# A hybrid attention, convolution and expert layer: one in-projection pass for blocks 4 to 7, and a last pass of only attention, output and peers

## The reference

```
h  = rmsnorm(x)
q, k, v, xc, B, C = split(h @ W_in)          # six parts of 512 columns
sb = stick_breaking(norm(q), norm(k), v)     # 8 heads x 64, causal, query blocks of 128
cv = B * causal_conv3(C * xc)                # 512 channels, 3 taps
x  = x + concat(rmsnorm(sb), rmsnorm(cv)) @ W_out
x  = x + peer(rmsnorm(x))
```

## Time and profile before

| | |
|---|---|
| median of 3 runs | 2881.12 us (2879.61 to 2883.12) |
| profiled execution | 2882.13 us, span 2880.3 us |
| busy: PE, DVE, ACT, POOL | 77%, 69%, 38%, 38% of the span |
| DMA | 1183.9 MB, mean 411 GB/s |
| mean granted TensorE clock | 0.894 |

### The profile page before, as it was taken

The page is one execution under the profiler, slowest core; times in us unless marked ns, Lnnn a source line. Parts: engine busy times, 40 slices in busy tenths (PEclk is TensorE's granted clock), DMA queues, the critical chain, the costliest instruction groups (busy, mean ns, idle before and its releaser), DMA issues. The chain is left out here.

```text
span 2880.3 us, 29917 instructions
## 1 busy us (share of the span) xinstructions
PE 2223.3 (77%) x9210; PEld 1010.4 (35%) x9210; DVE 1984.2 (69%) x4782; ACT 1094.2 (38%) x3164; POOL 1099.2 (38%) x1037
## 2 busy tenths in 40 slices
PE   9888989778986987778886888777898555555555
PEld 6535625333542343333542244333354111111111
DVE  3757766787667678787767666888676666666654
ACT  2333423552333335562333334666233322222222
POOL 0233433343333334443344333554334444434442
PEclk9999999989999998999998799999999787777787
DMA  9899999999999999999999999999999999999998
GB/s 389 333 418 412 398 419 419 417 403 416 387 422 420 419 419 414 414 419 412 407 421 421 420 411 419 406 421 414 419 408 421 419 421 417 420 418 415 418 421 353
DMA packets 178866, 1183.89 MB, mean 411 GB/s; under 512 B 19857, under 2 KB 21521, under 8 KB 47633
## 3 DMA queue, kind: packets, MB, share of 16 engines
q0 software_dynamic: 147456, 1073.81, 90.4%
q1 hardware_dynamic: 31248, 108.17, 9.5%
HBM read 1177.70 MB, written 4.19 MB: 410 GB/s over the span
## 5 line engine op out<-in xcount | busy, mean ns | idle before, releaser
L1471 DVE CUSTOM_DVE_ANT_0 ring<-ring,h2r 128x1024 f32<-128x1024 f32 x1024 | 1248.4, 1223 | 784.9 <-DMA ring<-table_uv,idx_t 778.9
L642 POOL DMA_INDIRECT ring<-table_uv,idx_t x1024 | 1097.3, 1072 | 1761.9 <-DVE dots L1471 1105.4
L910 PE MATMUL acc<-ring,wmask 128*64 128x512 f32 x4096 | 1199.0, 714 | 586.9 <-ACT wmask L1068 584.7
L910 PEld LDWEIGHTS acc<-ring,wmask 128*64 128x64 f32 x4096 | 282.2, 153 | 1299.9 <-ACT wmask L1068 859.9
L1063 ACT ACTIVATE dots<-dots 128x2 f32<-128x2 f32 x512 | 104.0, 203 | 1514.9 <-DVE dots L1471 1508.4
L1068 ACT ACTIVATE wmask<-gmask,dots 128x64 f32<-128x64 f32 x1024 | 300.3, 340 | 48.6 <-ACT dots L1063 1.5
L1056 ACT ACTIVATE gmask<-stack,gate_t 128x64 f32<-128x64 f32 x1024 | 293.1, 334 | 0.1
L665 PE MATMUL pt<-hT,w_held 128*128 128x256 f32 (+1 forms) x560 | 110.3, 347 | 0.0
L665 PEld LDWEIGHTS pt<-hT,w_held 128*128 128x128 f32 x560 | 89.0, 195 | 27.5 <-issue 20.2
L1063 ACT ACT_TABLE_LOAD x73 | 93.7, 1283 | 1.3
L656 PE MATMUL pz<-w_ring,hT 128*128 128x512 f32 x192 | 90.8, 615 | 0.0
(11 more groups left out here) (274 smaller groups left out, 2167.8 us busy)
## 6 DMA issues: line engine op xcount, KB each, us to landing
w_ring<-wstream SPq DMA_DIRECT2D x121, 512.0 KB
ring<-wstream SPq DMA_DIRECT2D x32, 512.0 KB, 12.2
ring<-table_uv,idx_t POOLq DMA_INDIRECT x1024
w_held<-wstream SPq DMA_DIRECT2D x11, 512.0 KB, 13.7
xs<-x_in_dram SPq DMA_DIRECT2D x8, 512.0 KB
h2r<-wstream SPq DMA_DIRECT2D x8, 512.0 KB
scores<-wstream SPq DMA_DIRECT2D x8, 512.0 KB
xs<-wstream SPq DMA_DIRECT2D x4, 512.0 KB
```

What stands on the lines that cost most here:

```text
L642: nc.gpsimd.indirect_dma_start(out=ring[:, cell(t):cell(t) + 2, :].rearrange("p c d -> p (c d)"), out_offset=None, in_=table, in_offset=ba ...
L910: mm = nc.tensor.matmul(acc[HALF * i:HALF * i + HALF, half * 512:(half + 1) * 512], wmask[:, slot, :], ring[:, cell(2 * p + i) + 1, half * ...
L1471: V.tensor_tensor_reduce(u, u, h2r[:, b % H_SLOTS, i, :], 1.0, 0.0, ALU.mult, ALU.add, dots[:, t % SLOTS:t % SLOTS + 1]).then_inc(dots_don ...
```

## The change

Pass 3 (`WIDE`) makes the in-projection of blocks 4 to 7. Each of its pieces 0 to 23 is done in four parts: the first two for blocks 4 and 5, the last two for blocks 6 and 7 (`AHEAD`). The order of its pieces is q, k, the convolution's, then v. Pass 4 (`LAST`) has only pieces 24 to 47.

The x of blocks 6 and 7 is loaded a second time, ahead, into room that two pieces of `w_held` had (`lent`: a second half of `cvT` and of `qT`); in passes 3 and 4 these two pieces, 37 and 38, are streamed, and in pass 3 so are 33 and 36. The transposed h of blocks 6 and 7 lies in the parts of `kT` and `vals_sb` that their own k and v will fill. The convolution works on 512 tokens at a time in pass 3, and one slot of the scores holds its input. Slots of the scores are numbered anew. Streamed pieces come to 103: 39 in pass 3, 15 in pass 4. The table puts the in-projection of pass 3 at ticks 286 to 366, its 16 attention passes at 369 to 442, its output pieces at 445 to 457 and its peer pieces from 465; pass 4 has its 16 attention passes at 524 to 670, output pieces at 676 to 699, and peer pieces from 715.

```diff
-WHEN = [(-1, -1, 10), (8, 66, 84), (72, 224, 262), (262, 470, 514), (521, 732, 775)]
+WIDE, LAST = 3, 4
+AHEAD = range(FIRST[LAST], BLOCKS)
+WHEN = [(-1, -1, 10), (8, 66, 84), (72, 224, 262), (262, 474, 514), (524, 732, 775)]
...
+ORDER = [list(range(PIECES)) for _ in SUPER]
+ORDER[WIDE] = [*range(PIECE_V), *range(PIECE_CONV, PIECE_OUT), *range(PIECE_V, PIECE_CONV), *range(PIECE_OUT, PIECES)]
+ORDER[LAST] = list(range(PIECE_OUT, PIECES))
...
+def parts_of(f, j):
+    return 4 if f == WIDE and j < PIECE_OUT else SUPER[f]
...
-    if j >= FIRST_HELD:
+    if j >= FIRST_HELD + LENT or j >= FIRST_HELD and f < WIDE:
         return "held", j - FIRST_HELD
...
+    if f == WIDE:
+        main += [(1.0, ("norm", b)) for b in AHEAD]
+        main += [pause(1), (6.0, ("root1", blocks[0])), pause(4)]
+        for pair in (blocks, AHEAD):
+            main += [(2.0, ("h_scale", b)) for b in pair]
+        for pair in (blocks, AHEAD):
+            main += [pause(1)] + [(3.0, ("h", b)) for b in pair] + [(3.0, ("hT", b)) for b in pair]
+        main += [pause(1)] + w(*range(PIECE_K)) + [pause(1)] + w(*range(PIECE_K, PIECE_V)) + [pause(1)]
+        main += [(1.0, ("qk_square", b)) for b in blocks] + w(12) + [(6.0, ("qk_root", blocks[0]))] + w(13)
+        main += [(3.0, ("qk_scale", b)) for b in blocks] + [pause(1)] + [(3.0, ("qk_turn", b)) for b in blocks]
+        main += [(1.0, ("qk_square", b)) for b in AHEAD] + w(14)
+        main += [(6.0, ("qk_root", AHEAD[0]))] + [(3.0, ("qk_scale", b)) for b in AHEAD] + [(8.0, ("conv", 0))]
+        for c in range(1, CH):
+            j = PIECE_CONV + 3 * c
+            main += w(j, j + 1, j + 2) + [(8.0, ("conv", c))]
+        main += w(*range(PIECE_V, PIECE_CONV)) + [pause(1)] + [(3.0, ("qk_turn", b)) for b in AHEAD]
+    elif f == LAST:
+        pass
...
             def front(f, name, *args):
+                if name == "ahead":
+                    sp.wait_ge(piece_done, done(f - 1, FIRST_HELD + LENT - 1))
+                    for i, b in enumerate(AHEAD):
+                        sp.dma_start(lent[i], x[b * P:(b + 1) * P, :]).then_inc(ahead_in, 16)
...
-                blocks = range(0 if begins else 1, n if ends else 1)
-                ks = range(0 if begins else KD // 2, KD if ends else KD // 2)
+                blocks = range(part, part + 1)
+                ks = range(part % n * KD // n, (part % n + 1) * KD // n)
...
+            def product_waits_ahead(f, j):
+                if j == PIECE_K:
+                    pe.wait_ge(q_kept, f + 2)
+                if j == PIECE_V:
+                    pe.wait_ge(cv_ready, 4 * f + 4)
...
                     act.wait_ge(piece_done, done(f, args[0]))
-                    wait(act, u_ready, 4 * f + c)
+                    wait(act, cv_ready if f == WIDE else u_ready, 4 * f + c)
```

More of the change, by code:

```diff
@@ L42 @@
 HELD = 11
+LENT = 2
 EARLY = 32
@@ L94, in cell, with done, made_by, made @@
     return -t * pow(U_HOLD, -1, TURN) % TURN
+ORDER = [list(range(PIECES)) for _ in SUPER]
+ORDER[WIDE] = [*range(PIECE_V), *range(PIECE_CONV, PIECE_OUT), *range(PIECE_V, PIECE_CONV), *range(PIECE_OUT, PIECES)]
+ORDER[LAST] = list(range(PIECE_OUT, PIECES))
+def done(f, j):
+    return sum(len(ORDER[g]) for g in range(f)) + ORDER[f].index(j) + 1
+def made_by(f):
+    return min(f, WIDE)
+def made(f):
+    return 4 if f == WIDE else SUPER[f]
+def made_to(f):
+    return min(BLOCKS, FIRST[made_by(f)] + made(made_by(f)))
+def parts_of(f, j):
+    return 4 if f == WIDE and j < PIECE_OUT else SUPER[f]
 def home(f, j):
-    if j >= FIRST_HELD:
+    if j >= FIRST_HELD + LENT or j >= FIRST_HELD and f < WIDE:
         return "held", j - FIRST_HELD
@@ L106, in home @@
         kind, room = divmod(j - FIRST_ROOM, 3)
-        if f <= room + 1:
+        if f <= min(room + 1, WIDE - 1):
             return ("vals", "keys")[kind], room + 1
     return "stream", 0
-STREAM = [(f, j) for f in range(len(SUPER)) for j in range(PIECES) if home(f, j)[0] == "stream"]
+STREAM = [(f, j) for f in range(len(SUPER)) for j in ORDER[f] if home(f, j)[0] == "stream"]
 PLACED = ([(0, j) for j in range(FIRST_HELD, PIECES)] + [(1, j) for j in range(SPARE)]
@@ L121, in piece_at, with front_head @@
     return j
+def front_head(n, blocks, pause, w):
+    main = [pause(1), (6.0, ("root1", blocks[0])), pause(6)]
+    main += [(2.0, ("h_scale", b)) for b in blocks] + [pause(2)]
+    main += [(3.0, ("h", b)) for b in blocks] + [(3.0, ("hT", b)) for b in blocks] + [pause(4)]
+    main += w(*range(PIECE_V)) + [(1.0, ("qk_square", b)) for b in blocks] + w(8)
+    main += [(6.0, ("qk_root", blocks[0]))] + w(9, 10) + [(3.0, ("qk_scale", b)) for b in blocks] + w(11)
+    return main
 def front_steps(f):
@@ L130, in w @@
     def w(*pieces):
-        if n == 1:
-            return [(piece, ("w", j)) for j in pieces]
-        return [(piece / 2, (half, j)) for j in pieces for half in ("v", "w")]
+        return [(piece / n, ("w", j) if part == parts_of(f, j) - 1 else ("v", j, part))
+                for j in pieces for part in range(parts_of(f, j))]
     def pause(ticks):
         return 0.0, ("pause", ticks)
-    main = [(1.0, ("norm", blocks[0]))]
-    for b in blocks[1:]:
+    main = [(0.0, ("ahead",))] if f == WIDE else []
@@ L140, in front_steps @@
+    main += [(1.0, ("norm", blocks[0]))] if f != LAST else []
+    for b in blocks[1:] if f != LAST else ():
         main += [pause(X_LATE if b >= X_SLOTS + 2 else 0), (1.0, ("norm", b))]
[L141 to L145, removed]
+    if f == WIDE:
[16 more added lines that the diff above has]
+        pass
+    else:
+        main += front_head(n, blocks, pause, w)
@@ L146, in front_steps @@
     conv = []
-    for c in range(CH):
+    for c in range(CH) if f < WIDE else ():
         j = PIECE_CONV + 3 * c
@@ L185, in front_steps @@
                 main += [(6.0, ("stick", *turns[s - 1]))]
-            if s == 1:
+            if s == 1 and f != LAST:
                 main += [(2.0, ("conv_sum",))]
@@ L791, in front @@
                     small_bank("sums")
-                    for t in range(n):
-                        for c in range(CH):
+                    rows, step = (CH, 256) if f < WIDE else (2, 512)
+                    for t in range(made(f)):
+                        for c in range(rows):
                             mm = nc.tensor.matmul(sum_cols[:, t:t + 1],
-                                                  squares[:, c * 256 + t * P:c * 256 + (t + 1) * P], ones[:],
-                                                  start=(c == 0), stop=(c == CH - 1))
+                                                  squares[:, c * step + t * P:c * step + (t + 1) * P], ones[:],
+                                                  start=(c == 0), stop=(c == rows - 1))
                     mm.then_inc(cv_ss, 1)
@@ L941, in front @@
                 i = b - b0
-                if name == "norm":
+                if name == "norm" and i > 1:
+                    act.wait_ge(ahead_in, 32)
+                    act.wait_ge(piece_done, done(f - 1, PIECES - 1))
+                    nc.scalar.activation(spare[i - 2], lent[i - 2], ACT.Square, accum_out=ss1[:, i:i + 1]).then_inc(x_squared, 1)
+                elif name == "norm":
                     act.wait_ge(x_in[b % 2], 16 * (b // 2 + 1))
@@ L1376, in front @@
                     wait(dve, cvT_ready, 4 * f + c)
+                    if f == WIDE and c > 1:
+                        step(V.tensor_tensor(squares[:, 0:wide], squares[:, 0:wide], squares[:, wide:2 * wide], ALU.add))
                     step(V.tensor_scalar(taps, u[:, 0:wide], tap(0), None, ALU.mult))
@@ L1406, in front @@
                         dve.wait_ge(added, 4 * b0 + n * order)
+                    elif f == LAST:
+                        for t in range(n):
+                            dve.wait_ge(x_in[(b0 + t) % 2], 16 * ((b0 + t) // 2 + 1))
                     for t in range(n):
```

206 lines of the change are left out of this document (127 added, 79 removed).

## The result

| | us, median (lowest to highest) | runs |
|---|---|---|
| before | 2880.28 (2877.30 to 2885.47) | 13 |
| after | 2886.98 (2883.45 to 2891.82) | 13 |

After over before is 1.0021 [1.0013, 1.0029]: 6.7 us slower, a small change, but its interval leaves out no change at all. The forecast was 2883.5, or 2.4 us slower. The profiled execution of after took 2891.82 us, 4.8 above its median; that of before lay 1.9 above its median of 13. So about 3 us of any difference between the two profiles is the choice of execution.

A forecast was written before the change was run, and what follows sets the result against it. The full DMA engines were taken as the bound: span 2880.3 - 20.2 + 20 + 3 - 0.5 = 2882.6, 2884.4 with 1.8 us around it; the execution lying 1.0 above the median, 2883.5 us. Range 2866 to 2899.

The forecast's parts named there:

- own case: Whole kernel: the saving is about offset by the wide in-projection and dense attention; 2876 to 2887 us, chance 0.38.
- The saving, 20.2 us: Streamed loads: 16 transfers of 512 KB fewer at 1.26 us each save 20.2 us (18.6 to 21.2).
- The wide in-projection, 20 us: Pass 3, ticks 286 to 366: TensorE's overrun of 22 us plus waits, less cover, loses 20 us (12 to 30).
- the sum of 254: Ticks 286 to 366: TensorE's pieces, mixes, turns and picks take 254 us, against 232 us for the DMA engines.
- The wait at the start: Start of pass 3's in-projection: TensorE waits 3.5 us for VectorE's dot and the copies of the transposed h.
- the one at the other end: End of pass 3's in-projection: blocks 6 and 7's first turn waits for ScalarE's v copies; with turns, 2.4 us over.
- the cover: The gather ring: TensorE may fall some 9 us behind, 8.1 beyond on time, before DMA idles.
- the rival: "The saving shows": in the wide in-projection, clock, pieces and 12 us of cover swallow TensorE's overrun; 2866 to 2871, chance 0.25.
- The dense attention, 3 us: Attention of blocks 4 and 5, pass 3: 4.06 ticks a pass instead of 5.3, VectorE at 92%; costs 3 us (0 to 12).
- Pass 4, -0.5 us: Pass 4 loses its in-projection, but spare engine time earns nothing while DMA is full: 0 to -0.5 us.
- a transfer costs its bytes: Rival for streamed loads: a transfer costs more than its bytes; at twice 1.26 us, 20 us more saved, 2863; chance 0.01.
- waits in the wide part: Rival for pass 3's in-projection: four-bank copies or a late conv step add waits, twice 4 us; 2891, chance 0.14.

The follow-up runs named there:

- dense kernel: Before, with pass 3's in-projection pieces stretched in the table so that its 16 attention passes stand as densely as in after; 2882.51 us against 2875.71, 1.0024.
- The pause: Three ticks of pause behind the first scores of passes 3 and 4: on after with 1.35-times-longer pieces 0.9983 of before, on after alone 1.0037.
- the kernel with 1.35: After, with pass 3's in-projection pieces 1.35 times as long in the table (ticks 285 to 376); 0.9975 of before, 0.9967 when repeated.

## Why the prediction came out as it did

The forecast's own case held: the saving is real, the wide in-projection eats it, and the net is small. The whole is 4.3 us off, as differences (+2.4 for +6.7), and 2886.98 stands at the very end of that case's 2876 to 2887. Its terms:

**The saving, 20.2 us: right.** Measured alone it is 17.0 (13.0 to 21.3), and the bytes agree: 8.4 MB less. In after, ticks 524 to 731 gave 26.5 us for 22 pieces (1.20 each), and two other stretches took 2.9 + 7.1 back for two loads and six pieces.

**The wide in-projection, 20 us: right cause, a few us too small.** It is 23.5 in ticks 286 to 366 (with 3 us of doubt from the choice of executions), and 21.3 came back when work was left out. Inside this sum two errors met, and that they nearly cancel is luck. First, TensorE was later than I had it. Its timeline in after, from the first piece to the last turn:

```profile
915.00 3.75 PE L747 MATMUL pz<-w_ring,hT 128*128 128x512 f32 x4 [3.35 <-issue]
918.68 2.89 PE L1024 MATMUL acc<-ring,wmask 128*64 128x512 f32 x8
921.50 1.98 PE L747 MATMUL pz<-w_ring,hT 128*128 128x512 f32 x4
...
1022.93 1.85 PE L742 MATMUL pt<-ident,rc 128*128 128x128 f32 x8 [2.42 <-ACT kT L1091]
1024.71 2.79 PE L1024 MATMUL acc<-ring,wmask 128*64 128x512 f32 x8
...
1046.56 3.68 PE L1024 MATMUL acc<-ring,wmask 128*64 128x512 f32 x8 [6.31 <-ACT wmask L1195]
...
1181.60 1.06 PE L742 MATMUL pt<-ident,rb 128*128 128x128 f32 x8 [0.49 <-ACT vals_sb L1081]
1184.11 1.06 PE L742 MATMUL pt<-ident,rc 128*128 128x128 f32 x8 [1.45 <-ACT kT L1091]
1185.10 1.94 PE L1024 MATMUL acc<-ring,wmask 128*64 128x512 f32 x8
```

From 915.0 to 1185.1 are 270.1 us. The idle times in them come to 2.42 + 6.31 + 0.49 + 1.45 = 10.7, so the work is 259.4, where I had 254. The excess of 5.4 is slower records: after the idle 3.35 us, four records take 3.75 instead of 1.98 and a mix 2.89 instead of 1.94, 2.7 together. After the idle 2.42 a turn takes 1.85 instead of 1.06 and a mix 2.79 instead of 1.94, 1.6 together, and after the 6.31 a mix takes 3.68, 1.7 more. That is some 6 in all, so at the full clock the work is about 253, and the sum of 254 was right. These are the granted clocks of the first two stretches, the last column but two (it reads 0.50 from 1046.5 to 1050.3 as well):

```profile
915.00:918.70 3.70, 3.70 (x6) 1.16 (x6) 2.44 (x5) 0.09 (x1) 1.48 (x2) 0.50 1.03 423
918.70:921.50 2.80, 2.80 (x9) 0.75 (x8) 2.54 (x12) 1.27 (x5) 0.00 (x0) 0.65 0.99 410
```

The wait at the start was priced well (3.35 for 3.5; its row names no releaser, but VectorE's last copy of the transposed h ended at 914.90) and the one at the other end nearly (1.94 for about 2.4). The two between were not in the sum at all. The longer, 6.31 us, goes through ScalarE to VectorE, here in after:

```profile
1036.34 1.22 DVE L1490 TENSOR_REDUCE ss<-rc 128x16 f32<-128x1024 f32 x1
...
1041.40 1.23 DVE L1606 CUSTOM_DVE_ANT_0 ring<-ring,h2r 128x1024 f32<-128x1024 f32 x1
...
1045.62 0.20 ACT L1190 ACTIVATE dots<-dots 128x2 f32<-128x2 f32 x1 [7.80 <-DVE dots L1606]
```

Between 1036.3 and 1041.4 VectorE makes `qk_root` (two sums of squares and the root), and no dot, though gathers have landed (the dot at 1041.40 waits for nothing). The busy sums had told me that VectorE has room; a step of 5 us in one piece is not seen in them.

The copies of q, which I gave nothing, did cost nothing: ScalarE waits 12.69 us for TensorE's piece until 955.82, and TensorE idles nowhere near it.

Second, the cover is larger than 8.1. The lateness is 3.35 + 270.1 - 235.2 (before's length for the same ticks) = 38 us, where the forecast's terms come to 27.9, and 24 to 27 were lost, so some 11 to 15 were covered. The mixes show it: the pair whose last dot ended at 971.8 was mixed at 988.0, 16.2 us later, and near the end of the stretch the pair of tick 363 was mixed 14.9 us after its dot. That is about the 12 us that I had given to the rival. TensorE wasn't late all through: the pair ahead of the 6.31 us was mixed 1.9 us after its dot. That the 6.31 us costs time in after was not tested by itself; with half the work the same 6.31 stands in the trace, and 415 GB/s beside it.

**The dense attention, 3 us: the term whose mechanism failed.** Measured in before alone it is 6.8 (4.3 to 9.8). I had spread VectorE's work over all ticks (92%) and priced the density. The dense kernel's trace shows no price for density over 144 us, and a few us at each place where one phase hands over to the next. In after, of the 10.4 us lost from 1152 on, 4.7 stand in one slice at the attention's beginning (some 3 more belong to the end of the in-projection):

```profile
1188.00:1200.00 12.00, 10.52 (x39) 4.79 (x37) 5.93 (x8) 9.22 (x18) 3.86 (x5) 0.72 0.73 253
```

There the last turns, the first two scores and a double mix (5.56 us at 1193.25) follow each other, ScalarE being busy for 9.2 of 12 us. Half the work on TensorE did not remove this (4.7 us lost in its stretch from 1152). I have argued its cause from the timeline and not shown it.

**Pass 4, -0.5 us: neither confirmed nor refuted.** Its 22 pieces would have given 25.5 to 29.3 us by the forecast's prices and gave 26.5, so the rest is -1.0 to +2.8. It does have an edge that I hadn't seen, 3.5 us in the slice at 1614. The pause removed it, but ticks 524 to 731 became only 0.3 us shorter in the kernel with 1.35 and 1.6 in after, so how much time that edge costs isn't known.

**The rivals.** The saving did not show; a transfer costs its bytes (1.06 us) and not twice that; waits in the wide part exist about as long as that rival had them (8.7 us of TensorE's), though the longer one came from another step (`qk_root`), and under a larger cover.

The parts, taken at their measured values, come to -17 to -20 + 21 to 24 + 7, or 8 to 14, and the kernel measured 6.7. The intervals of the parts (some 3 to 5 us each) hold this difference, and those of whole kernels are the ones to trust. Open are what makes the edge where the output begins, what the one at the beginning costs, and what the wait for `hT` does.

## What to carry to other kernels

Where a full DMA queue sets the pace, a saved transfer is worth its bytes, but only if no engine falls behind the ring for longer than the ring covers. Sum that engine's work in the table's ticks against the gathers' time in them, and widen the ticks until it fits: here 11 more ticks turned 0.2% slower into 0.25 to 0.33% faster. In a hand-written order look for collisions at the edges of phases (a shared PSUM bank, two first steps side by side, one long step on the engine that frees buffers). Mean loads don't show them. Moving one step moves others (here a pause of three ticks took two from the in-projection), so look again at each edge, and at the place of the steps that you didn't mean to move. And look in the trace of the kernel you edit whether the wait is there that the edit is to remove.

## What was unexpected of the hardware

- The DMA share hides loss: in after a share of 0.95 went with 373 GB/s and 0.88 with 334, where 1.01 goes with 417. That is 6% and 13% less in the share, but 11% and 20% less in the rate. Why the busy share falls by less than the rate isn't shown here.
- After 3.35 us of idling TensorE's first four records took 3.75 us, which later take 1.98 (the granted clock reads 0.50 in this stretch, its lower level of 1.2 GHz, and 1.00 from 921.5 on), and the mix behind them 2.89 instead of 1.94, just where the densest stretch began. The idle times of 2.42 and 6.31 us had slower records behind them as well. The three together idled for 12.1 us and cost 6.1 more in slow records. Not every low stretch goes with such a wait: in the dense kernel in before the clock had fallen before the 4.23 us of waiting began.
- With mixes 12 to 17 us late the DMA engines still moved 334 GB/s, four fifths of the full rate. TensorE was busy for all of these 62 us and the lateness no longer grew, so gathers came at TensorE's pace there.
